# Second block, rotations beside dense attention: root of the first pair, and steps and turns of the third and fourth tile, moved to other parts of the order

## The reference, cut to what matters

```python
aq = apply_rope_2(rms_norm(aq.reshape(B, S, A_HEADS, HEAD_DIM), a_q_norm), cos, sin)
ak = apply_rope_2(rms_norm(ak.reshape(B, S, A_HEADS, HEAD_DIM), a_k_norm), cos, sin)
...
ya = sparse_attention(aq, ak, av, iq, ik, iw, k_sel).reshape(B, S, D_A)
...
yb = diff_attention(bq, bk, bv, lam)
```

## Time and profile before

| | us |
|---|---|
| median of 3 runs (2330.34 to 2333.05) | 2330.41 |
| the profiled execution, its own time | 2336.28 |
| its span, first to last instruction | 2334.6 |
| TensorE busy | 2221.2 (95%) |
| VectorE busy | 1240.0 (53%) |
| ScalarE busy | 844.0 (36%) |
| GpSimd busy | 354.4 (15%) |
| mean granted TensorE clock | 0.980 |

### The profile page before, as it was taken

One profiled execution on the slowest core, in us unless ns is written; L12 is line 12 of the kernel. 1 busy time (PEld: TensorE's weight loads), 2 busy tenths in 40 slices (PEclk: granted clock), 3 DMA queues, 4 the chain that ended last, 5 costly groups with the idle time before them and its releaser, 6 DMA issues.

```text
span 2334.6 us, 28101 instructions
## 1 busy us (share of the span) xinstructions
PE 2221.2 (95%) x10765; PEld 1683.0 (72%) x10765; DVE 1240.0 (53%) x2363; ACT 844.0 (36%) x1486; POOL 354.4 (15%) x273
## 2 busy tenths in 40 slices
PE   7999999779898999999999999999999999999999
PEld 4885677643335776777888888887677787888887
DVE  4743445651226777665654434459766755443442
ACT  4444442421112446434332222344554433332221
POOL 0111023000001455331000000025443200000000
PEclk9999898879999999999999999999999999999999
DMA  8216310289996232221323323232222123323322
GB/s 302 60 55 216 118 37 10 105 334 410 409 409 234 74 90 55 73 76 42 99 91 100 99 90 105 82 99 73 73 62 75 56 72 100 100 90 100 100 81 81
DMA packets 175580, 288.01 MB, mean 123 GB/s; under 512 B 13486, under 2 KB 125656, under 8 KB 175448
## 3 DMA queue, kind: packets, MB, share of 16 engines
q1 hardware_dynamic: 173152, 278.73, 35.5%
q0 software_dynamic: 1152, 4.19, 0.5%
q10 hardware_dynamic: 1144, 3.29, 0.4%
HBM read 281.98 MB, written 4.19 MB: 123 GB/s over the span
## 4 chain that ended last, share of the span: by engine, by line
PE 79%; DVE 10%; DMA 5%; ACT 3%; issue 2%; SPq 1%; POOL 0%; DVEq 0%; ACTq 0%
PE PS L677 21%; PE PS L679 20%; PE PS L678 20%; PE PS L1451 3%; PE PS L2440 3%; PE PS L2479 2%; PE PS L1433 2%; PE PS L2499 1%; PE PS L1443 1%; PE PS L1618 1%; PE PS L1628 1%; DMA AR<-in_w_mod_dram 1%; SPq L3634 1%; PE PS L1100 1%; DMA ONCE<-in_w_gate_dram 1%
## 5 line engine op out<-in xcount | busy, mean ns | idle before, releaser
L677 PE MATMUL PS<-OPH,WHI 128*128 128x512 f32 x1224 | 499.1, 408 | 13.9 <-DVE AR L1288 5.0
L679 PE MATMUL PS<-OPH,WLO 128*128 128x512 f32 x1224 | 481.9, 394 | 0.0
L678 PE MATMUL PS<-OPL,WHI 128*128 128x512 f32 x1224 | 480.9, 393 | 0.0
L628 ACT ACTIVATE WHI<-RAW 128x1024 fp32r<-128x1024 f32 (+2 forms) x282 | 292.8, 1041 | 457.3 <-PE PS L679 449.1
L649 DVE TENSOR_TENSOR WLO<-RAW,WHI 128x1024 fp32r<-128x1024 f32 (+1 forms) x187 | 224.2, 1201 | 373.8 <-ACT WHI L628 373.7
L665 POOL TENSOR_TENSOR WLO<-RAW,WHI 128x1024 fp32r<-128x1024 f32 (+1 forms) x95 | 229.5, 2418 | 952.9 <-ACT WHI L628 946.9
L677 PEld LDWEIGHTS PS<-OPH,WHI 128*128 128x128 f32 x1224 | 232.1, 190 | 81.2 <-issue 28.0
L679 PEld LDWEIGHTS PS<-OPH,WLO 128*128 128x128 f32 x1224 | 232.0, 190 | 50.4
L678 PEld LDWEIGHTS PS<-OPL,WHI 128*128 128x128 f32 x1224 | 232.6, 190 | 43.5 <-issue 1.0
L677 PE MATMUL PS<-WHI,OPH 128*128 128x512 f32 (+2 forms) x568 | 228.4, 402 | 7.9 <-DVE OPL L2140 2.4
L679 PE MATMUL PS<-WHI,OPL 128*128 128x512 f32 (+2 forms) x568 | 216.0, 380 | 0.0
(11 more groups left out here) (446 smaller groups left out, 3255.1 us busy)
## 6 DMA issues: line engine op xcount, KB each, us to landing
RAW<-in_w_in_dram SPq DMA_DIRECT2D x102, 512.0 KB, 3.7
RAW<-in_w_ffn_in_dram SPq DMA_DIRECT2D x88, 512.0 KB, 3.5
RAW<-in_w_ffn_out_dram SPq DMA_DIRECT2D x40, 512.0 KB, 3.4
RAW<-in_w_mod_dram SPq DMA_DIRECT2D x36, 512.0 KB, 4.6
ONCE<-in_w_down_dram SPq DMA_DIRECT2D x35, 512.0 KB, 15.8
RX<-in_w_gate_dram SPq DMA_DIRECT2D x33, 512.0 KB, 15.6
RAW<-in_w_out_dram SPq DMA_DIRECT2D x24, 512.0 KB, 3.5
ONCE<-in_w_up_dram SPq DMA_DIRECT2D x20, 512.0 KB, 14.9
```

The source lines that it names most:

```text
L628: hi.up(A.e.activation(q.fhi, q.flat, ACT.Copy), ("w", q.i))
L677: T.e.matmul(o, a[0], b[0], start=first, stop=False)
L678: T.e.matmul(o, a[0], b[1], start=False, stop=False)
L679: return T.e.matmul(o, a[1], b[0], start=False, stop=last)
```

## The change

It touches when the steps are issued, in both layers. With `rope_part(y, lags)` each tile t has a lag of its own (None: not due); the part is 12 + 16a + 3t + lag.

- turn and copy: lags (9, 9, 9, 9) become (9, 9, 12, 12). For `aq`: parts 21, 24, 27, 30 become 21, 24, 30, 33; for `ak`: 37, 40, 43, 46 become 37, 40, 46, 49. Part 49 belongs to the gate columns, so `pe_between` gets an explicit call there.
- ScalarE's root: pair 0 and 1 in part 17 instead of 18 (33 instead of 34), behind the squares of the same part; pair 2 and 3 stays at 24 (40).
- rope: lags 2, 2, 3, 3, so `aq` parts 14, 17, 21, 24 instead of 14, 17, 20, 23 (`ak` 30, 33, 37, 40).
- rope's end: lags 7, 7, 9, 9, so `aq` parts 19, 22, 27, 30 instead of 19, 22, 25, 28 (`ak` 35, 38, 43, 46).

```diff
         def turn_due(y):
-            return each_third(y, 9)
+            return rope_part(y, (9, 9, 12, 12))
+
+        def rope_part(y, lags):
+            for a in range(2):
+                for t in range(4):
+                    if lags[t] and y == 12 + 16 * a + 3 * t + lags[t]:
+                        return a, t
...
+                        if (g, n, j) == (0, 0, 0):
+                            pe_rope_turns(first + 8)
...
-                at = each_third(y, 3)
-                if at and at[1] % 2:
-                    act_rope_root(first + 4 * at[0] + at[1] - 1, 2)
-                at = each_third(y, 2)
+                at = rope_part(y, (2, 2, 2, 2))
                 if at:
                     act_rope_squares(first + 4 * at[0] + at[1])
+                at = rope_part(y, (None, 2, None, 3))
+                if at:
+                    act_rope_root(first + 4 * at[0] + at[1] - 1, 2)
...
-                at = each_third(y, 7)
+                at = rope_part(y, (7, 7, 9, 9))
                 if at:
                     dve_rope_end(first + 4 * at[0] + at[1])
-                at = each_third(y, 2)
+                at = rope_part(y, (2, 2, 3, 3))
                 if at:
                     dve_rope(first + 4 * at[0] + at[1])
```

## The result

| | before | after |
|---|---|---|
| median of 8 runs, us | 2331.61 (2325.29 to 2336.89) | 2345.23 (2339.89 to 2349.04) |
| ratio | | 1.0059, 95% interval 1.0045 to 1.0074 |
| profiled execution's own time, us | 2336.28 | 2342.59 |

The change costs 13.8 us of 2331.6 (10.5 to 17.3). The forecast was +6.6 with a range to 2339.0 (+8.6): the direction was right, the size was not, and the result lies outside the range.

What follows compares the result with a forecast made beforehand. TensorE was taken to bound the kernel, its gains and losses arriving one for one. The terms -1.9 -0.8 +1.2 +2.8 +2.0 gave +3.3 us per layer, +6.6 on 2330.4: 2337.0 us, 8-in-10 range 2329.0 to 2339.0.

Steps and rivals of the forecast that it cites:

- Rival A: Both layers: all five terms come as worked out, +6.6 us, time 2337.0 us; chance 0.52.
- Term 1: Unit 7: transposed weights directly follow the turn, without their idle wait for VectorE's "least"; -1.9 us per layer.
- Term 2: Unit 8: the wait of the transposed weights for "least" halves but doesn't vanish; -0.8 us per layer (0 to -1.6).
- Term 3: Unit 9: second score tile late, its bank's copy behind a rope held by GpSimd; +1.2 us per layer (0 to 1.5).
- Term 4: Unit 12: second score tile 2.9 us late, its bank's copy behind VectorE's block end and rope; +2.8 us (2.6 to 3.1).
- Term 5: Unit 16: GpSimd begins 0.16 us before VectorE's L880, which is held ahead of "least"; +2.0 us per layer (0 or 2.1).
- Units 10, 11, 13 to 15 at 0: These units of each layer: moved turns and later ends cost or win TensorE nothing; 0 us.
- Rival B: Unit 16: VectorE begins first, so L880 isn't held; +1.3 us per layer, time 2333.0 us; chance 0.20.
- Rival C: Unit 12's second score tile: the bank of turn 3 isn't needed late; time 2325.0, 2327.4 or 2331.4 us; chance 0.18.
- D: Whole stage: nothing visible, waits are moved and VectorE's idle time swallows the new ones; time 2330.4 us; chance 0.10.
- the likeliest case: All five terms in both layers, time 2337.0 us, own range 2335.5 to 2339.0 us; chance 0.52.

Runs made afterwards that it cites:

- the last version: Fastest version (aq's changed steps, its turns and copies in parts 22, 26, 29, 32) with ak's turns and copies also one part later; ratio 0.9986 (0.9968 to 1.0005).

## Why the prediction was right in its direction and wrong in its size

**What bounds the stage** held: the gains and losses of TensorE there add up to 13.4 us, against 13.8 measured (10.5 to 17.3), and behind the stages nothing changed. Rival A's mechanisms all came, each at its place.

**Term 1, -1.9:** measured -2.0 (7.87 to 5.88). Right, though the root's part in it was nothing; the ropes do it alone.

**Term 2, -0.8:** measured -0.95. The second wait halved and didn't vanish; in the trace it stands mostly at the turn (0.60 us for the rope's end) and not at the weights.

**Term 3, +1.2:** measured +1.18 (7.06 less 5.88, which is the 6.31 of before less the turn's 0.43; with the copy first it took 5.87). Right, by the held L859. I had it at 1.8 us (A+8.4 to A+10.2), it took 1.88.

**Term 4, +2.8:** the step that failed. The tile was 2.96 us late, as I had it, but unit 12 grew by 5.78 and 4.23 us. "The tile is 2.9 us late, and its cost is its lateness": that sentence rested on a lateness of 0.7 us (889.72), behind which the clock stays up. Behind this one TensorE ran at half its clock for about 6.8 us in one layer and 3.4 in the other. Without any wait the unit takes 6.88 us (as with `ak`'s turns one part later), so 9.84 with the late tile; the clock adds 3.1 and 1.6 us. The bound of 3.1 had no room for that. No row of before has such a fall in this stage, though there is a wait of 1.84 us in it. The fully idle part of the wait in unit 12 was 1.84 us as well, so the idle time that a row shows doesn't tell the two apart.

**Term 5, +2.0:** the hold, its cause and even the order came as worked out (0.11 us instead of 0.16), and 2.14 us is its size without a fall of the clock. With it the unit lost 3.7: the same step as in term 4 was left out here, and the bound of 2.1 had no room for it either. Rival B, which rested on that margin and on the page "Perfetto Trace Analysis" of the Trainium skill, section "GPSIMD Engine Instruction", was wrong: unit 16 lost its 2 us in both layers of all four profiles (of three kernels) that had this order. The start times were good enough for 0.1 us here, whatever the spans are worth. The Trainium skill's page "SBUF — State Buffer", section "Who interferes with whom", fits what was seen: 2.83 us with GpSimd first, 0.69 with VectorE first, everything else equal.

**Units 10, 11, 13 to 15 at 0:** right, but for 0.26 us gained in unit 14, where a short wait vanished.

**Rival C** was wrong: VectorE's order put the copy behind the block end. **D** was wrong.

**The range** of the likeliest case, 2335.5 to 2339.0, isn't what "terms 2 to 5 at their bounds" give. Those bounds add up to -0.9 and +4.8 us per layer, 2328.6 to 2340.0. The result lies outside either.

So without the clock the terms come to -2.0 -0.95 +1.18 +2.66 +2.14 and -0.26 for unit 14, +2.8 us per layer where I had 3.3. The 2.66 is an estimate, 9.84 less the 7.18 of before: the lateness of 2.96 less the 0.30 us wait at the next turn that it hides. The stages grew by 7.5 and 5.9: 4.7 and 3.1 us are the lower clock, which no term held.

The Trainium skill's page "TensorE: Matmul & The Clock Gate", section "Part 1: The HAM clock gate (the "warmup" mystery)", says that a gate sets the array's clock by how busy TensorE has lately been, which I had left out of the sum. The traces agree in that every fall seen in these two stages follows a wait with 1.84 to 1.95 us of idle time, and they show the two levels; they do not settle why the same wait of 1.9 us ended in a fall in one kernel and not in the other.

## What to carry to other kernels

Where banks are dealt in program order, moving one step changes who gets which bank from there on: count the banks on, and for each one ask what stands ahead of its reader in the reader's own queue (here a block end, a rope, an instruction held by GpSimd). A wait of two or three microseconds that is added to TensorE must be costed with and without a fall of its clock, since the fall can cost as much as the wait (here 1.6 or 3.1 us on waits of 2 to 3). A step that needs its bank back soon belongs behind the operand that depends on it and ahead of the next long item of the reader, and the copy that frees a bank goes first in its part.

## What the runs showed of the hardware that I had not expected

- Behind a late score tile (2.96 us) the granted clock went to half for about 3.4 or 6.8 us, one size in each layer in all four kernels that had that wait (unit 12 at 11.4 and 13.0 us); in three of them the first layer had the longer one, in one the second. In these two stages there were these two sizes and nothing between; the first cost 1.6 us, the second 3.1.
- The wait of 1.9 us in unit 16 made the clock fall in the changed kernel and with the copy first (17.1 us), and not in the kernel with the turn in part 32 (15.49 us), in two profiles and both layers each. In the last version, the wait of 1.95 us in unit 14 ended in a fall in both layers. What decides it is open. In the changed kernel and in the one with the turn in part 32, units 13 to 15 have the same lengths, so the difference must lie further ahead of the wait; I did not try to vary it.
- One more ScalarE instruction of 0.5 us, by which GpSimd starts behind VectorE instead of ahead of it, took 3.7 us off a unit.
- The end of a hold can be read off closely. In and around both stages of all thirteen profiles, every L859, L872 and L880 of VectorE that began 0.06 to 2.05 us behind the start of a single low half (L665) ended 0.54 to 0.56 us behind its end (86 cases). Every one that began 0.11 to 0.66 us ahead of it took its usual 0.64 to 0.70 us (134 cases). The low half then reads longer where the lead is short: 2.83 us at 0.11 us of lead, 2.39 at 0.65.
